# Retention with its decays computed two heads ahead and its gated tiles rounded and split inside the head loop; context tiles of two joints scaled ahead of the latent root

## The reference, cut to what matters

```python
x = x + g1 * rmsnorm(y_lat, norm_g[i, 1])                  # end of a half layer: "post" norm
h = modulate(rmsnorm(x, norm_g[i, 2]), sh2, sc2)           # start of the next: "norm"
...
xc = xc + cg1 * rmsnorm(y_ctx, norm_g[i, 1])               # the same for the context
hc = modulate(rmsnorm(xc, norm_g[i, 2]), csh2, csc2)
...
# retention, for each of 8 heads and two directions d, q, k: 128 wide, v: 256 wide
s = einsum('bhqd,bhkd->bhqk', qf, kf) * decay_intra        # decay = exp(lg * distance), masked
o = einsum('bhqk,bhkv->bhqv', s, vf) + (the same with the context's keys and values)
...
on = (o - mean(o)) * lax.rsqrt(var(o) + EPS) * gn_g
y = (silu(g) * on) @ w_out
```

## Time and profile before

| | |
|---|---|
| Median of 3 runs | 2088.14 us (2082.11 to 2090.48) |
| Profiled execution | 2090.16 us, of which 2088.3 us from the first to the last instruction |
| PE, weight loads, DVE | busy 97%, 88% and 78% of that span |
| ACT, POOL | busy 56% and 7% |
| Mean granted TensorE clock | 0.993 |
| First joint (m = 0) | PE 1184.2 to 1206.3 us for the latents' half |
| Second joint (m = 1) | PE 1569.3 to 1583.0 us for its three abreast |
| Retention loop | PE 1732.5 to 1829.2 us |

### The profile page before, as it was taken

The page is one execution under the profiler, slowest core; times in us unless marked ns, Lnnn a source line. Parts: engine busy times, 40 slices in busy tenths (PEclk is TensorE's granted clock), DMA queues, the critical chain, the costliest instruction groups (busy, mean ns, idle before and its releaser), DMA issues.

```text
span 2088.3 us, 37048 instructions
## 1 busy us (share of the span) xinstructions
PE 2017.8 (97%) x13975; PEld 1827.4 (88%) x13975; DVE 1624.2 (78%) x2668; ACT 1170.3 (56%) x2116; POOL 148.0 (7%) x233
## 2 busy tenths in 40 slices
PE   6999999999999999998999999999999999999998
PEld 6988999999988999997876888888887888998997
DVE  7888879966688879978687889786979436657983
ACT  6757756645557756646636455352544226656862
POOL 0100000100000000004000300001102000000000
PEclk9999999999999999999999999999999999999999
DMA  9866548765766557866341234546634223244553
GB/s 363 284 204 210 180 173 273 274 223 170 241 217 207 184 170 265 302 237 213 119 164 55 101 131 157 196 140 234 219 133 142 91 92 100 91 152 136 196 184 110
DMA packets 106624, 383.03 MB, mean 183 GB/s; under 512 B 11504, under 2 KB 16128, under 8 KB 105184
## 3 DMA queue, kind: packets, MB, share of 16 engines
q1 hardware_dynamic: 77584, 280.21, 39.3%
q0 software_dynamic: 25792, 94.31, 13.6%
q10 hardware_dynamic: 3088, 6.29, 0.9%
HBM read 379.71 MB, written 1.05 MB: 182 GB/s over the span
## 4 chain that ended last, share of the span: by engine, by line
PE 74%; DVE 13%; issue 4%; ACT 4%; DMA 3%; POOL 0%; POOLq 0%; DVEq 0%; SPq 0%; ACTq 0%
PE ps L1104 18%; PE ps L1108 17%; PE ps L1107 17%; DVE ring_l L2394 3%; DVE ada_junk L2417 3%; PE ps L1125 3%; PE ps L1129 3%; PE ps L1130 3%; PE ps L1147 2%; DMA work<-adas_in 2%; PE ps L1150 2%; PE ps L1151 2%; ACT ring_r L1734 2%; PE ps L1684 1%; DMA ring<-tape_in 1%
## 5 line engine op out<-in xcount | busy, mean ns | idle before, releaser
L1104 PE MATMUL ps<-part,ring_l 128*128 128x256 f32 (+1 forms) x3373 | 1012.4, 300 | 8.3 <-DVE ring_l L2394 8.1
L1108 PE MATMUL ps<-part,ring_r 128*128 128x256 f32 (+1 forms) x3373 | 1005.4, 298 | 0.0
L1107 PE MATMUL ps<-part,ring_r 128*128 128x256 f32 (+1 forms) x3373 | 1004.6, 298 | 0.0
L2394 DVE TENSOR_TENSOR ring_l<-ring,ring_r 128x1024 fp32r<-128x1024 f32 x514 | 626.6, 1232 | 142.8 <-ACT ring_r L1734 140.5
L1734 ACT ACTIVATE ring_r<-ring 128x1024 fp32r<-128x1024 f32 x514 | 533.6, 1056 | 332.4 <-DMA ring<-tape_in 235.6
L1104 PEld LDWEIGHTS ps<-part,ring_l 128*128 128x128 f32 x3373 | 635.2, 188 | 40.5 <-issue 8.8
L1107 PEld LDWEIGHTS ps<-part,ring_r 128*128 128x128 f32 x3373 | 635.4, 188 | 25.3
L1108 PEld LDWEIGHTS ps<-part,ring_r 128*128 128x128 f32 x3373 | 634.6, 188 | 21.6
L2417 DVE SCALAR_TENSOR_TENSOR ada_junk<-work 128x1024 bf16<-128x1024 f32 x272 | 334.2, 1229 | 51.4 <-DMA work<-adas_in 39.7
L1147 PE MATMUL ps<-part,ring_l 128*128 128x256 f32 (+1 forms) x472 | 144.7, 307 | 20.1 <-DVE part L2394 10.6
L1150 PE MATMUL ps<-part,ring_r 128*128 128x256 f32 (+1 forms) x472 | 141.1, 299 | 0.0
(11 more groups left out here) (287 smaller groups left out, 2114.2 us busy)
## 6 DMA issues: line engine op xcount, KB each, us to landing
ring<-tape_in SPq DMA_DIRECT2D x514, 512.0 KB, 3.4
work<-adas_in POOLq DMA_DIRECT2D x176, 512.0 KB, 4.6
work<-ada_first_in SPq DMA_DIRECT2D x8, 1024.0 KB, 17.5
work<-bias_in ACTq DMA_DIRECT2D x1, 2048.0 KB, 7.9
x<-x_t_in SPq DMA_DIRECT2D x1, 1024.0 KB, 7.5
work<-cond_in POOLq DMA_DIRECT2D x1, 1024.0 KB, 8.7
x<-ctx_in ACTq DMA_DIRECT2D x1, 1024.0 KB, 9.3
x<-dist_in ACTq DMA_DIRECT2D x1, 1024.0 KB, 6.4
```

The source lines that it names most:

```text
L1104: mm = pe.matmul(dst, lhsT=wl, rhs=mr, start=(k == 0), stop=False)
L1107: pe.matmul(dst, lhsT=wr, rhs=mr, start=False, stop=False)
L1108: mm = pe.matmul(dst, lhsT=wr, rhs=ml, start=False, stop=(k == len(moving) - 1))
L2394: return dve.tensor_tensor(dst, whole, rounded_part.bitcast(F32), ALU.subtract)
```

## The change

Four edits, all in the second block.

1. **Joints.** After `norm_out`, DVE scales 5 of the 8 context tiles (`CONTEXT_EARLY`) before it waits for the latents' new root; the other 3 stay beside latent tiles 0 to 2. For m = 0 it also splits one panel (the fifth of the convolution) beside latent tile 3, where all of them came behind tile 7 before.
2. **Decays.** Those of heads 0 and 1 are computed during the value streams c = 1 and 2, and in the loop those of head i + 2.
3. **Panels at the values.** Ahead of the last value stream's copies ACT rounds two more panels and DVE splits one more.
4. **Gated tiles.** They get a new place in the values of their own head, `ret_v`, which are dead by then; so rounding and splitting go into the loop (head i - 3), and the norm of a head comes one step earlier (i - 2). PE's variance goes from the end of a step to behind its scores.

The diff, cut to its core:

```diff
+CONTEXT_EARLY = 5
+DECAYS_IN_V = (1, 2)
@@ (bank order and PE's loop alike)
                 ret_scores(i)
+                if 0 <= i - 2 < H:
+                    ret_variance(i - 2)
                 ret_gate(2 * i)
                 ret_values(i - 1)
                 ret_gate(2 * i + 1)
-                if 0 <= i - 2 < H:
-                    ret_variance(i - 2)
@@ places
-        gated_r = at_r(U2, 2 * KD, T2)[:, :, 0:T]
-        gated_l = [values_r[:, i % 2, i // 2 * RV:i // 2 * RV + RV] for i in range(RVT)]
+        gated_l, gated_r = ([values_r[:, 2 * part:2 * part + 2, h * RV:(h + 1) * RV] for h in range(H)] for part in range(2))
@@ ACT
+            for c in range(4):
+                if c in DECAYS_IN_V:
+                    decay_powers(DECAYS_IN_V.index(c))
+                if c == 3:
+                    round_panels(READ2["ret_v2_3"] + RING + 2)
                 for b in range(4):
...
+                    if c < 3:
+                        finished2(f"ret_v{c}_{b}")
@@
             for i in range(H + 1):
-                if i + 1 < H:
-                    decay_powers(i + 1)
                 if i < H:
                     ret_sigma(2 * i)
+                if 0 <= i - 2 < H:
+                    ret_root_of(i - 2)
+                if i + 2 < H:
+                    decay_powers(i + 2)
+                if 0 <= i - 3 < H:
+                    round_gated(i - 3)
                 if 0 <= i - 1 < H:
                     copy_ret_o(i - 1)
                 if i < H:
                     ret_sigma(2 * i + 1)
-                if 0 <= i - 2 < H:
-                    ret_root_of(i - 2)
-            for h in range(4):
-                round_gated(h)
             round_panels(READ2[f"ret_g{RVT - 1}"] + RING)
+            round_gated(H - 2)
             ret_root_of(H - 1)
-            for h in range(4, H):
-                round_gated(h)
+            round_gated(H - 1)
@@ DVE, joints
-                norm_in(m + 2, 0, kind_in, chunk, lambda k: context_scaled(m, kind_out, k))
+                for k in range(CONTEXT_EARLY):
+                    context_scaled(m, kind_out, k)
+                def beside_latents(k):
+                    if CONTEXT_EARLY + k < KD:
+                        context_scaled(m, kind_out, CONTEXT_EARLY + k)
+                    if m == 0 and k == 3:
+                        split_panels(DEPTH * PANELS_1 + START2["conv0_0_0"] + CONV_ABREAST[0])
+                norm_in(m + 2, 0, kind_in, chunk, beside_latents)
@@ DVE, values
                 ahead2(f"ret_v{c}_0")
+                if c in DECAYS_IN_V:
+                    decays(DECAYS_IN_V.index(c))
+                if c == 3:
+                    split_panels(DEPTH * PANELS_1 + READ2["ret_v2_3"] + RING)
@@ DVE, loop
                     decay_scores(i)
                     ret_silu_of(2 * i)
+                if 0 <= i - 2 < H:
+                    ret_norm(i - 2)
+                if i + 2 < H:
+                    decays(i + 2)
                 if 0 <= i - 3 < H:
-                    ret_norm(i - 3)
-                if i + 1 < H:
-                    decays(i + 1)
+                    rest_gated(i - 3)
                 if i < H:
                     ret_silu_of(2 * i + 1)
```

More of the change, by code:

```diff
@@ L390, in order_block2 @@
         if i < H:
-            o += [f"ret_score{i}_0", f"ret_score{i}_1", f"ret_g{2 * i}"]
+            o += [f"ret_score{i}_0", f"ret_score{i}_1"]
+        if 0 <= i - 2 < H:
+            o.append(f"ret_var{i - 2}")
+        if i < H:
+            o.append(f"ret_g{2 * i}")
         if 0 <= i - 1 < H:
@@ L1703, in _ @@
                     ret_gate(2 * i + 1)
-                if 0 <= i - 2 < H:
-                    ret_variance(i - 2)
-            gated = [(gated_r[:, k, :], gated_l[k]) for k in range(RVT)]
+            gated = [(gated_r[k // 2][:, k % 2, :], gated_l[k // 2][:, k % 2, :]) for k in range(RVT)]
             project2_abreast([f"out2_0_{f}" for f in range(ABREAST)], gated, lambda k: ret_parted(k),
@@ L2313, in _ @@
                 finished2(f"ret_qk{f}")
[L2314 to L2321, removed]
             def decay_powers(h):
@@ L2331, in decay_powers @@
                                    scale=misc_of("log_decay")[:, d * H + h:d * H + h + 1]).then_inc(decay_exp.sem, 1)
-            decay_powers(0)
+            for c in range(4):
[3 more added lines that the diff above has]
+                    round_panels(READ2["ret_v2_3"] + RING + 2)
+                for b in range(4):
+                    act.wait_ge(*done2(f"ret_v{c}_{b}"))
+                    for a in range(2):
+                        n = 8 * c + 2 * b + a
+                        act.activation(ret_v[:, b, (2 * c + a) * RV:(2 * c + a + 1) * RV], bank2(f"ret_v{c}_{b}")[:, a * RV:(a + 1) * RV],
+                                       ACT.Copy, accum_out=v_sums[:, n:n + 1]).then_inc(ret_v_made.sem, 1)
+                    if c < 3:
+                        finished2(f"ret_v{c}_{b}")
             def ret_sigma(f):
@@ L3213, in _ @@
                         dve.tensor_scalar(v, v, v_means[:, n:n + 1], None, ALU.add).then_inc(v_centred.sem, 1)
-            dve.wait_ge(loaded["mask"], 16)
-            decays(0)
             def ret_silu_of(f):
@@ L3246, in rest_gated @@
                 dve.wait_ge(*ret_round(h))
-                for k in range(2 * h, 2 * h + 2):
-                    rest(gated_l[k], ret_g[:, k, :], gated_r[:, k, :]).then_inc(ret_parted.sem, 1)
+                for k in range(2):
+                    rest(gated_l[h][:, k, :], ret_g[:, 2 * h + k, :], gated_r[h][:, k, :]).then_inc(ret_parted.sem, 1)
             for i in range(H + 1):
@@ L3253, in _ @@
                     ret_silu_of(2 * i)
+                if 0 <= i - 2 < H:
+                    ret_norm(i - 2)
+                if i + 2 < H:
+                    decays(i + 2)
                 if 0 <= i - 3 < H:
-                    ret_norm(i - 3)
-                if i + 1 < H:
-                    decays(i + 1)
+                    rest_gated(i - 3)
                 if i < H:
                     ret_silu_of(2 * i + 1)
-            rest_gated(0)
-            rest_gated(1)
-            ret_norm(H - 2)
-            rest_gated(2)
-            rest_gated(3)
+            rest_gated(H - 2)
             ret_norm(H - 1)
-            for h in range(4, H):
-                rest_gated(h)
+            rest_gated(H - 1)
             for f in range(3, KD + 1):
```

6 lines of the change are left out of this document (3 added, 3 removed).

## The result

The changed kernel took 2076.01 us (median of 9 runs, 2068.61 to 2078.25), the kernel before 2088.14 us (9 runs, 2082.11 to 2093.95). The ratio is 0.994, with a 95% interval of 0.9925 to 0.9954: about 12 us faster, where 12.4 were predicted. The profiled execution took 2078.25 us, with 2076.5 from the first to the last instruction and a mean clock of 0.996. PE is busy 97% of the span as before, and DMA is no part of what follows.

A forecast was written before the change was run, and what follows sets the result against it. PE was taken to set the pace, so only its waits and half clock could be won: 3.7 + 2.7 + 4.4 + 1.6 = 12.4 us off the median of 2088.14 gives 2075.7 us, range 2069 to 2084.

The forecast's parts named there:

- Retention, start: Start of retention: PE's 2.33 us panel wait and 1.36 us of half clock behind it go, 3.7 us.
- end (2.7): Ahead of retention's output projection: PE's 2.68 us wait for the first gated tile goes, 2.7 us.
- Retention, middle: Head loop: PE's moved variance waits for nothing, as ACT is done 1.1 us in time; costed at nothing.
- The rival that was to end slower: Head loop: ACT becomes the bound and PE waits in 7 steps; 2103 us at 5 us longer a head, chance 0.05.
- First joint: First joint: the 2.83 us panel gap goes and the clock stays full, 4.4 us.
- bounds of 1.0 and 5.1: First joint's gain: 1.0 us if half clock stays, 5.1 if PE never waits for tile 4.
- POOL ends near 1196.6: First joint: POOL does 6 sums and 5 additions in 10 us, so the context's sums can start at once.
- Second joint: Second joint: latent tile 6 starts 0.8 us earlier and POOL's 0.76 us gap goes, 1.6 us.
- nine more instructions at 0.92: Second joint: DVE, sharing with POOL, has nine instructions at 0.92 us to the rest of tile 6, near 1579.7.
- the 1.8 of the first: Rival: retention wins, the joints hardly (1.0 and 0.8 us) as contention only moves; 2079.9 us, chance 0.25.
- the 10.1 of the second: Rival: the joints run at PE's pace, 5.1 and 5.0 us, as DVE slips between POOL's instructions; 2071.6 us, chance 0.17.
- the third's 1.3 us a pair: Rival at the joints: DVE and POOL run one after the other in full, 1.3 us a pair; 2084.1 us, chance 0.05.

The follow-up runs named there:

- e2: The kernel before with only the joints' edit; 2079.66 us, ratio 0.9972 to the kernel before.
- e7: The changed kernel with each decay power of heads 2 to 7 computed twice by ACT; 2084.97 us, ratio 0.9977 to the kernel before.
- e6: The changed kernel without the panel split beside latent tile 3 at the first joint; 2073.10 us, ratio 0.9927 to the kernel before.
- e12: The changed kernel run again unaltered, for a second trace; 2074.30 us, ratio 0.9927 to the kernel before.
- e11: The changed kernel with 7 instead of 6 pairs of bridging matmuls ahead of the last feed-forward; 2078.50 us, ratio 0.9948 to the kernel before.
- e1: The changed kernel with the joints as in the kernel before, so retention's edits alone; 2078.20 us, ratio 0.9967 to the kernel before.
- e5: The changed kernel with DVE splitting the panels behind the last latent tile only after POOL's last sum; 2069.77 us, ratio 0.9909 to the kernel before.
- e3: The changed kernel with all 8 context tiles scaled early instead of 5; 2070.09 us, ratio 0.9941 to the kernel before.
- e10: The changed kernel without early scaling, keeping the panel beside latent tile 3; 2081.01 us, ratio 0.9955 to the kernel before.
- e8: The changed kernel with 8 tiles early at the second joint, no panel at tile 3, later panels behind POOL's last sum; 2076.18 us, ratio 0.9932 to before.

## Why the prediction came out

Retention came out as worked out. The joints' sum came out by luck: 4.4 + 1.6 = 6.0 was forecast and 2.8 + 2.7 = 5.5 found, with one term 1.6 us too large and the other 1.1 too small.

- **Retention, start (3.7) and end (2.7).** Right. 3.8 and 3.2 side by side, less the 0.1 and 0.3 that e2 shows too: 3.7 and 2.9. Gap and half clock went together, and nothing else came late.
- **Retention, middle (0).** Right, and so is the reason: e7 measured the 1.1 us as 1.2. The rival that was to end slower would have needed 4.4 us more work a head.
- **First joint (4.4).** Too large: 3.2, 3.3, 3.1, 2.7 and 1.5 in five traces of the same code, 2.8 in the mean, inside the bounds of 1.0 and 5.1. The step that failed is "POOL ends near 1196.6". In the time of the kernel before it ended near 1199.3 (15.1 us behind the first tile, 1184.16 in the earlier trace rows). Its eleven instructions took 13.4 us (1181.07 to 1194.52) and not the 10 that I gave them: three met a panel (0.8 more each), and one waited 1.29 for a square. The 1.71 beside a panel stands in the earlier trace rows, and I used it for DVE's side and not for POOL's. Two more points fell. The early split panel isn't what takes the 2.83 us gap away: without it the gap is 0.66 us (e6). And the clock doesn't always stay full without that gap: e12 has 6.8 us of half clock behind a wait for POOL, and 1.5 us won. Nor did that half clock cost the 3.4 us of my lower bound: e12 stands 1.6 us behind e11, which has the same wait at full clock. PE stood still for 1.0 of those 6.8 us, and e11 at full clock waited another 0.84 us for the context's first tile, which e12 did not.
- **Second joint (1.6).** Too small: 2.9 and 3.1 where both have the half clock of 1560.8, 2.6 to 2.8 where neither has (e1 against e2, e5, e6, e11, e12). The step "nine more instructions at 0.92" was too dear: from DVE's first shared instruction (1564.75) to the end of the rest of tile 6 (1572.2) they took 7.5 us and not 8.3, since a pair repeats every 0.88 and one of the nine met no instruction of POOL. PE started tile 6 9.6 us behind the first tile where I had 10.5, and POOL's 0.76 came on top as counted.
- **Sum.** 3.7 + 2.9 + 2.8 + 2.7 = 12.1 by the means, and 12.1 between the medians. That the two agree so closely is luck again: the median of the kernel before moved from 2086.08 to 2089.81 us between the experiments. The rivals: the joints won 5.5 us and not the 1.8 of the first or the 10.1 of the second; the third's 1.3 us a pair is not seen, a pair takes 0.88 to 0.92; and in the loop PE never waited for ACT.

## What to carry to other kernels

Scaling that needs only an old root belongs into the idle time ahead of the new one; check that the last engine of the chain (here POOL with its sums), and not only the next, has its data. When something is moved between the links of a chain over three engines, count what each of them does behind it: a 1.2 us panel for DVE held up ACT's rounding, ACT's square, POOL's sum and so PE, though PE never waited for the panel. And read a short stage from more than one execution: the same 3.27 us wait with or without half clock behind it made a difference of 1.6 us here (e12, e11) with the same code at the joint.

## What the runs showed of the hardware

**DVE and POOL on two SBUF inputs.** Alone, DVE starts one every 0.40 us and POOL needs 0.73 (e5). Together a pair takes 0.88 to 0.92, less than 1.13, so they don't exclude each other over their whole length; but once in step, each waits for the other's every instruction. At the first joint POOL's first sum, started 0.02 to 0.03 us behind a DVE instruction, was done after 1.05 us in six traces and after 3.39 in three, where five DVE instructions went ahead of it; at the second joint it took 1.05 in all seven traces with such a start. The Trainium skill, page "SBUF — State Buffer", section "Who interferes with whom", says that issue order decides who blocks. DVE was first in all these traces, and POOL did wait; but issue order doesn't tell the 1.05 from the 3.39, and four of the five DVE instructions of the 3.39 started after POOL's. What decides is open. That the block lasts for the whole instruction, the 0.88 us pair doesn't bear out.

**Two cadences of the same matmuls.** PE without any wait, at clock 1.00, in the last feed-forward of before, after and e1:

```profile
core 0: us, PE busy (x), PEclk, DMA share, GB/s
1900.00:2000.00 100.00, 100.00 (x885) 1.00 0.58 194
```

```profile
1885.00:1985.00 100.00, 100.00 (x852) 1.00 0.57 189
```

```profile
1885.00:1985.00 100.00, 100.00 (x885) 1.00 0.60 195
```

885 matmuls of 128x256 in 100 us, or 852: one every 113.3 or every 117.8 ns. 1100 of them took 124.67 us in before, e1, e2 and e3 and 129.56 in the ten others, nothing between. Other stages have both as well (in most of the stretch from 926 to 957 us before has 113.3, after 117.8). The cadence often changes at a wait of PE, but not only there: the trace after goes from 91 matmuls in 10 us to 87 at 427.2 us with no wait between (same columns).

```profile
411.00:421.00 10.00, 10.00 (x91) 1.00 0.82 279
427.50:437.50 10.00, 10.00 (x87) 1.00 0.83 283
```

The cadence makes the +4.7 us of the first section. The other two have other causes. Of the -4.8, 1.7 is a stretch of half clock from 973.7 us on that of the two only before has, and 1.5 is this wait, which before has and none of the other 13 traces:

```profile
1074.85 1.99 PE L1558 MATMUL ps<-work 64*128 64x512 f32 x8 [1.45 <-DVE work L3072]
```

The other 1.6 had come together in small steps by 920 us.

The +1.4 are three waits for DVE in the trace after, in code that no edit touches:

```profile
1517.94 0.50 PE L1150 MATMUL ps<-part,ring_l 128*128 128x512 f32 x1 [0.29 <-DVE part L2401]
...
1521.04 0.50 PE L1150 MATMUL ps<-part,ring_l 128*128 128x512 f32 x1 [0.75 <-DVE part L2401]
...
1523.76 0.50 PE L1150 MATMUL ps<-part,ring_l 128*128 128x512 f32 x1 [0.37 <-DVE part L2401]
```

The 4.9 us between the two cadences are half of the 10 us over which runs of one kernel spread; how much of the spread they make isn't shown, since a kernel has one trace (the changed kernel two). What sets the cadence stays open: e11 moved the restart ahead of this stage and settled nothing.

**The granted clock.** Of waits of 2.8 to 4.1 us at the first joint four had 6.8 us of half clock behind them (before, e1, e10, e12), one 3.4 (e2) and one none (e11, 3.27 us); no wait between tiles, of up to 1.94 us (e8), had any. At the second joint the same 1.49 us wait for ACT ahead of L1440 came with 3.4 us of half clock in seven traces and without in the other seven; it is worth 1.6 to 1.9 us.
